# Turning both residuals on VectorE instead of TensorE, in a one-core hybrid decoder block (Trainium2)

## The reference

```python
m = (sigmoid(ga) * (y_h @ w_branch_hgrn) + sigmoid(gb) * (y_a @ w_branch_dsa))
h = h + m @ w_out
u = rmsnorm(h, ffn_norm_w)
a = causal_dwconv(u @ w_ffn_gate, ffn_conv_w, ffn_conv_b)
h = h + (silu(a) * (u @ w_ffn_up)) @ w_ffn_down
return rmsnorm(h, final_norm_w)[:, N_META:]
```

## Time and profile before

| | us |
|---|---|
| median of 3 runs | 1599.75 (1599.56 to 1600.13) |
| the profiled execution | 1599.79 |
| its span | 1598.0 |
| PE busy | 1586.3 (99%) |
| DVE busy | 972.0 (61%) |
| ACT busy | 708.5 (44%) |
| POOL busy | 116.0 (7%) |
| DMA, mean | 182 GB/s |

### The profile page before, as it was taken

The page is one execution under the profiler, slowest core; times in us unless marked ns, Lnnn a source line. Parts: engine busy times, 40 slices in busy tenths (PEclk is TensorE's granted clock), DMA queues, the critical chain, the costliest instruction groups (busy, mean ns, idle before and its releaser), DMA issues.

```text
span 1598.0 us, 29335 instructions
## 1 busy us (share of the span) xinstructions
PE 1586.3 (99%) x12162; PEld 1527.7 (96%) x12162; DVE 972.0 (61%) x1126; ACT 708.5 (44%) x746; POOL 116.0 (7%) x165
## 2 busy tenths in 40 slices
PE   9999999999999999999999999999999999999998
PEld 8999999999999999999999999998889999999886
DVE  7655878853355566786656666665445666666453
ACT  6433554544443345654345455544333334334342
POOL 1000140000000002352220000000000000000000
PEclk9999999999999999999999999999999999999999
DMA  7755555555555553576555565645455555565551
GB/s 244 227 179 164 158 165 179 178 179 179 179 189 180 159 159 119 191 246 203 177 191 191 172 195 165 203 162 204 173 198 181 188 180 187 174 194 198 196 210 54
DMA packets 244998, 290.36 MB, mean 182 GB/s; under 512 B 5697, under 2 KB 231218, under 8 KB 244530
## 3 DMA queue, kind: packets, MB, share of 16 engines
q1 hardware_dynamic: 238146, 278.78, 53.4%
q0 software_dynamic: 2176, 6.34, 1.2%
q10 hardware_dynamic: 4608, 4.23, 0.8%
HBM read 283.02 MB, written 6.32 MB: 181 GB/s over the span
## 4 chain that ended last, share of the span: by engine, by line
PE 99%; DVE 0%; ACT 0%; DMA 0%; issue 0%; SPq 0%; DVEq 0%
PE ps L654 25%; PE ps L655 24%; PE ps L656 24%; PE ps L1092 5%; PE ps L1095 5%; PE ps L1094 5%; PE ps L1041 2%; PE ps L1039 2%; PE ps L1040 2%; PE ps L817 1%; PE ps L685 0%; PE ps L792 0%; PE ps L934 0%; PE ps L1031 0%; PE ps L827 0%; PE ps L1079 0%
## 5 line engine op out<-in xcount | busy, mean ns | idle before, releaser
L654 PE MATMUL ps<-u_hi,w_hi 128*128 128x258 f32 (+2 forms) x2936 | 839.1, 286 | 0.0
L655 PE MATMUL ps<-u_lo,w_hi 128*128 128x258 f32 (+2 forms) x2936 | 831.4, 283 | 0.0
L656 PE MATMUL ps<-u_hi,w_lo 128*128 128x258 f32 (+2 forms) x2936 | 831.1, 283 | 0.0
L1447 DVE TENSOR_TENSOR w_lo<-raw,w_hi 128x2048 fp32r<-128x2048 f32 x259 | 598.1, 2309 | 353.6 <-ACT w_hi L1136 353.1
L1136 ACT ACTIVATE w_hi<-raw 128x2048 fp32r<-128x2048 f32 x259 | 495.9, 1916 | 565.1 <-PE ps L656 393.4
L654 PEld LDWEIGHTS ps<-u_hi,w_hi 128*128 128x128 f32 x2936 | 554.0, 189 | 5.1 <-DVE z_qf L1560 2.5
L655 PEld LDWEIGHTS ps<-u_lo,w_hi 128*128 128x128 f32 x2936 | 554.0, 189 | 0.3
L656 PEld LDWEIGHTS ps<-u_hi,w_lo 128*128 128x128 f32 x2936 | 553.8, 189 | 0.0
L1092 PE MATMUL ps<-w_hi,hid_hi 128*128 128x512 f32 x352 | 137.8, 391 | 0.0
L1095 PE MATMUL ps<-w_lo,hid_hi 128*128 128x512 f32 x352 | 137.1, 389 | 0.0
L1094 PE MATMUL ps<-w_hi,hid_lo 128*128 128x512 f32 x352 | 137.0, 389 | 0.0
(11 more groups left out here) (299 smaller groups left out, 1307.4 us busy)
## 6 DMA issues: line engine op xcount, KB each, us to landing
raw<-in_w_in_dram SPq DMA_DIRECT2D x47, 2048.0 KB, 8.5
raw<-in_w_ffn_gate_dram SPq DMA_DIRECT2D x22, 2048.0 KB, 8.1
raw<-in_w_ffn_up_dram SPq DMA_DIRECT2D x22, 2048.0 KB, 8.1
raw<-in_w_ffn_down_dram SPq DMA_DIRECT2D x20, 2048.0 KB, 7.6
raw<-in_w_out_dram SPq DMA_DIRECT2D x8, 2048.0 KB, 8.9
raw<-in_w_branch_hgrn_dram SPq DMA_DIRECT2D x8, 1024.0 KB, 5.5
raw<-in_w_branch_dsa_dram SPq DMA_DIRECT2D x8, 1024.0 KB, 8.8
gate_spill<-gate_st ACTq DMA_DIRECT2D x32, 129.0 KB, 3.9
```

What stands on the lines that cost most here:

```text
L654: mm(acc, w_hi[s][:, k, :], mov_hi(k), start=(k == first), stop=False)
L655: mm(acc, w_hi[s][:, k, :], mov_lo(k), start=False, stop=False)
L656: ins = mm(acc, w_lo[s][:, k, :], mov_hi(k), start=False, stop=(k == last))
L1447: v.tensor_tensor(w_lo[m % 4][:], raw[(m // 2) % 2][:, :, P * (m % 2):P * (m % 2) + P], w_hi[m % 4][:].bitcast(F32), ALU.subtract).then_in ...
```

## The change

Four things are edited.

1. **x is turned by DVE.** DMAs bring x as 32x32 blocks placed so that DVE's 32x32 block transpose gives the whole turn (`x_sh`, 16 DMAs of 32x8x32 for four units, `x_quad`; the two meta tokens as `xm_sh`, 4 DMAs). `x_sh[1]` lies over `ya_hi`, so its first load waits for the end of `U_MERGE`. PE's 48 turning matmuls go, and DVE adds bank and turned x in place of the copy.
2. **h is turned back by DVE.** DVE block-transposes each unit of h into a ring of four (`h_sh`); ACT stores it, one unit later, with 4 DMAs of 32x8x32 to a DRAM tensor `h_spill` that then holds h with tokens as rows. POOL loads it into `h_tok` after the stage, and DVE adds it at the end of the first `U_DOWN`. PE's 32 turning matmuls go.
3. **Merge entry.** ACT takes two sigmoids ahead of the weights, DVE takes the first sum ahead of the weight rest. The merge and out loops of ACT, DVE and POOL are written out instead of looped.
4. **Start.** ACT rounds the key panel's halves at n = 10 and 15 instead of 14 and 16, DVE makes the first rest at n = 12 instead of 15, the first half of the first query unit is rounded after the last x piece, and PE has one more warm-up matmul.

```diff
-        x_st = [at(f"x_st{a}", BIAS + 3072 * a, [P, 3, 256]) for a in range(2)]
+        x_sh = [at(f"x_sh{a}", (BIAS, R[4])[a], [P, 4, SEQ]) for a in range(2)]
+        xt = [at(f"xt{a}", BIAS + 4096 + 1024 * a, [P, SEQ]) for a in range(2)]
+        xm_sh = at("xm_sh", R[7] + 5184, [P, KT, 32])
...
+        x_blocks = x[0].rearrange("(b j) (k a i) -> a j k b i", j=32, a=4, i=32)
+        meta_blocks = meta_tokens.rearrange("j (k a i) -> a j k i", a=4, i=32)
+        h_blocks = h_spill.rearrange("(b j) (k a i) -> a j k b i", j=32, a=4, i=32)
...
+            def x_quad(q):
                 for a in range(4):
+                    for k in range(4):
+                        pool.dma_start(x_sh[q % 2][32 * a:32 * a + 32, k, :].rearrange("j (b i) -> j b i", i=32),
+                                       x_blocks[a, :, 4 * q + k, :, :]).then_inc(x_sh_in[q % 2], 16)
...
+            pool.wait_ge(o_gated, HEADS)
+            steps.link(pool, pool.memset(ssq[:], 0.0))
+            pool.wait_ge(projected, U_MERGE)
+            pool.wait_ge(ya_ready, 9)
+            pool.memset(xm_sh[:], 0.0).then_inc(xm_zeroed, 1)
+            x_quad(0)
+            pool.wait_ge(xm_zeroed, 1)
+            for a in range(4):
+                pool.dma_start(xm_sh[32 * a:32 * a + 2, :, :], meta_blocks[a, T0:META, :, :]).then_inc(xm_in, 16)
+            pool.wait_ge(projected, U_OUT)
+            x_quad(1)
+            for n in range(16):
+                if n in (4, 8):
+                    pool.wait_ge(xt_turned, n)
+                    x_quad(n // 4 + 1)
                 if n == 15:
                     pool.tensor_copy(spare[:, 5:6], ssq[:, 0:1]).then_inc(ssq_ready, 1)
                 squares(n, slice(n, n + 1), n == 15)
...
+            warm_up(1)
...
-                    if u % 2 == 0:
-                        pe.wait_ge(x_st_in[u // 2], 32 * i + 32)
                     pe.wait_ge(out_free, 4 * i + (u + 1))
-                    bank = ps[6 + u % 2]
-                    for t in range(3):
-                        ins = mm(bank[:, P * t:P * t + P], x_st[u // 2][:, t, P * (u % 2):P * (u % 2) + P], ident[:],
-                                 is_transpose=True, start=(t == 0), stop=False, skip_group_check=True)
-                    ins.then_inc(xt_turned, 1)
...
-                        if f == 0 and half == 0:
-                            residual(c, j % 2, t)
...
-                if n == 2 * EARLY:
+                if n == EARLY + 3:
                     act.wait_ge(key_in, 16)
                     round_keys(slice(0, 8))
-                if n == 2 * EARLY + 2:
+                if n == 2 * EARLY + 1:
...
+            gate_sigmoid(0)
+            gate_sigmoid(1)
+            ahead(U_MERGE)
+            for n in range(16):
+                ahead(U_MERGE + n + 1)
+                act.wait_ge(m_sum, n + 1)
...
+            def store_turned(u):
+                act.wait_ge(h_turned, u + 1)
+                for a in range(4):
+                    act.dma_start(h_blocks[a, :, u, :, :],
+                                  h_sh[u % 4][32 * a:32 * a + 32, :].rearrange("j (b i) -> j b i", i=32))\
+                        .then_inc(h_out[u % 4], 16)
...
+            for u in range(16):
+                m, h = U_OUT + u, h_res[:, u, :]
+                if u == 0:
+                    dve.wait_ge(xm_in, 64)
+                    v.transpose(xm[:].rearrange("p k t -> p (k t)"), xm_sh[:].rearrange("p k t -> p (k t)"))\
+                        .then_inc(xm_turned, 1)
+                    dve.wait_ge(xm_turned, 1)
+                if u % 4 == 0:
+                    dve.wait_ge(x_sh_in[(u // 4) % 2], 256 * (u // 8) + 256)
+                v.transpose(xt[u % 2][:], x_sh[(u // 4) % 2][:, u % 4, :]).then_inc(xt_turned, 1)
+                dve.wait_ge(xt_turned, u + 1)
+                dve.wait_ge(projected, m + 1)
+                v.tensor_tensor(h[:, 0:2], ps[6 + u % 2][:, 0:2], xm[:, u, 0:2], ALU.add)
+                v.tensor_tensor(h[:, 2:TQ], ps[6 + u % 2][:, 2:TQ], xt[u % 2][:], ALU.add).then_inc(out_free, 1)
...
+                v.transpose(h_sh[u % 4][:], h[:, 2:TQ]).then_inc(h_turned, 1)
+                ahead(m + 1, m + 1)
```

More of the change, by code:

```diff
@@ L339, in hybrid_block @@
         m_ready = sem("m_ready")
-        x_st_in = [sem("x_st_in0"), sem("x_st_in1")]
+        x_sh_in = [sem("x_sh_in0"), sem("x_sh_in1")]
+        xm_zeroed = sem("xm_zeroed")
+        xm_in = sem("xm_in")
+        xm_turned = sem("xm_turned")
         xt_turned = sem("xt_turned")
+        h_turned = sem("h_turned")
+        h_out = [sem(f"h_out{a}") for a in range(4)]
+        h_in = sem("h_in")
         ssq_ready = sem("ssq_ready")
@@ L601, in _ @@
                 gate_pair(n, n)
[L602 to L606, removed]
+            for n in range(4):
                 scale_gates(n, 16)
[L608 to L613, removed]
-                for a in range(4):
[L615 to L620, removed]
+            for n in range(4, 16):
+                pool.wait_ge(m_ready, n - 3)
+                gate_pair(n, n % 4)
+                if n > 4:
+                    scale_gates((n - 1) % 4, 16 * ((n - 1) // 4) + 16)
+            scale_gates(3, 64)
+            def x_quad(q):
+                for a in range(4):
+                    for k in range(4):
+                        pool.dma_start(x_sh[q % 2][32 * a:32 * a + 32, k, :].rearrange("j (b i) -> j b i", i=32),
+                                       x_blocks[a, :, 4 * q + k, :, :]).then_inc(x_sh_in[q % 2], 16)
             def squares(n, tile, last=False):
@@ L644, in _ @@
                 squares(n, slice(n, n + 1), n == 15)
+            pool.wait_ge(u2h_ready, 16)
+            pool.wait_ge(u2l_ready, 16)
+            for a in range(4):
+                pool.wait_ge(h_out[a], 4 * 64)
+            pool.wait_ge(ssq_ready, 2)
+            for c in range(2):
+                pool.dma_start(h_tok[c][:], h_spill[:, 1024 * c:1024 * c + 1024].rearrange("(t p) n -> p t n", p=P))\
+                    .then_inc(h_in, 16)
         @block.tensor
@@ L1037, in _ @@
                             pe.wait_ge(m_ready, k + 1)
[L1038 to L1042, removed]
+                        ins = products(ps[6 + u % 2][:, 0:TQ], n % 4, (k,), lambda k: m_hi[:, k, :],
+                                       lambda k: m_lo[:, k, :])
                     ins.then_inc(projected, 1)
@@ L1822, in _ @@
                         if u == 3:
+                            if half == 0:
+                                for r in range(4):
+                                    dve.wait_ge(h_out[r], 4 * 64)
                             low(0)
@@ L1849, in add @@
                     bank = ps[down_bank(half, c, u, t)][:].rearrange("p (g c) -> p g c", c=P)
-                    if half == 0:
-                        v.tensor_copy(h, bank).then_inc(down_added, 1)
-                    else:
-                        v.tensor_tensor(h, bank, h, ALU.add).then_inc(down_added, 1)
+                    v.tensor_tensor(h, bank, h, ALU.add).then_inc(down_added, 1)
                 for j in range(1, FH - 3):
```

108 lines of the change are left out of this document (42 added, 66 removed).

## The result

| us | before | changed |
|---|---|---|
| median | 1599.71 (1599.56 to 1600.13, 6 runs) | 1588.92 (1588.72 to 1589.34, 6 runs) |
| span of the profiled execution | 1598.0 | 1587.0 |
| PE / DVE / POOL busy | 1586.3 / 972.0 / 116.0 | 1576.2 / 978.5 / 146.8 |

The ratio is 0.9932, interval 0.9922 to 0.9943: 10.8 us faster. The prediction said 1594.3 (5.5 faster) and a range that began at 1589.0, 0.1 us above the result.

A forecast was written before the change was run, and what follows sets the result against it. PE, 99% busy with almost no stall to win, was taken as the bound. Terms -8.8 - 0.5 + 1.8 + 2.2 - 0.2 = -5.5 us on 1599.79 gave 1594.3, range 1589 to 1600.5.

The forecast's parts named there:

- Turns taken off PE, -8.8: Out and first down stages: 16 turns of x at 0.33 us and 8 banks of h at 0.44 save 8.8 us.
- Merge entry, -0.5: Merge start: PE's 1.1 us stall goes, 0.6 is given back for second release and late panel; net -0.5 us.
- the second release: Merge entry: two weight rests delay the second bank's release to 668.2, while PE asks at 668.0.
- the late panel: Merge entry: SyncE's next weight panel leaves 2.4 us later; 0.6 us given back for this and the second release together.
- The first sum, +1.8: Out stage: x loads land late, the first sum frees its bank at 756.7, PE asks at 754.9: 1.8 us stall.
- The loop and the `ssq` matmul, +2.2: Out stage: VectorE's loop takes 5.7 us a unit, so PE waits 2.2 us at the sum-of-squares matmul.
- Start, -0.2: Kernel start: the wait for the keys' first rest goes against x pieces held up by the earlier rounding; -0.2 us.
- a part of a rival: Start, within "All is hidden": the added matmul brings PE's quicker turning pace sooner, saving 0.8 us.
- All is hidden: Rival, out stage: meta tokens land early or the loop takes 5.45, no stall comes; 1589.7 to 1590.3 us, chance 0.2.
- POOL's issues: Rival, ahead of the first sum: x loads cost more than 0.79 us an issue; about 1607 at 1.6, chance 0.08.
- The DMA engines: Rival, out stage: 28,672 small pieces fill the DMA engines and panels come late, deciding at 24 ns each; chance 0.07.
- VectorE was not the bound: Rival, out stage: VectorE's loop takes 6.1 us, the last sum comes 6 us later; about 1600 us, chance 0.15.

The follow-up runs named there:

- e3: The changed kernel with the merge entry as before (weight roundings and rest ahead of the first sigmoid and sum): 1589.63 us.
- e11: The changed kernel with 9 more clearings of the meta buffer on POOL ahead of the first loads of x: 1595.49 us.
- e4: The changed kernel with 16 more clearings of the meta buffer on POOL ahead of the first loads of x: 1599.07 us.
- e6: The changed kernel with the block transpose of x done twice in each output-stage unit: 1594.82 us.
- e1: The changed kernel without the one added warm-up matmul: 1589.46 us.
- e2: The changed kernel with the key panel rounded and split where it was before, the added warm-up matmul kept: 1589.12 us.
- e8: The changed kernel with a second store of each turned unit of h, by POOL into another DRAM tensor: 1603.69 us.

## Why the prediction was wrong

The profiled execution was 11.0 us shorter, the forecast said 5.5. Of the 5.5 between them 4.0 are two waits that did not come, 0.8 the turns, 0.5 the start and 0.2 the merge entry.

- **Turns taken off PE, -8.8: right, sized too small.** By the traces 5.72 and 3.85, together 9.6; by the runs 9.5. The 0.33 and 0.44 of the chain are the turns' own starts. The distance between the same matmul of two units, 6.12 against 5.76, shows 0.36 for x, and the down stage 0.48 a bank.
- **Merge entry, -0.5: nearly right.** 0.73 by the trace, 0.5 by e3. The stall went as worked out, the second release cost its 0.2, and the 0.4 for the late panel did not come.
- **The first sum, +1.8: this is the step that failed.** POOL's issue was priced at 0.79 by a load over 128 partitions; the load over 32 took 0.58. Over 16 issues that is 3.3 us. The scaling ended 1.6 us sooner than reckoned, in part since start and merge had gained more, and the landing took 4.8 instead of 6.0. VectorE's own part took 1.3 us for the 1.15 assumed. Together the first sum came 5.9 us sooner than predicted (750.3 for 756.15): not 2 us late but with 3.2 us in hand. e11 and e4 show the slack, and the price once it is spent.
- **The loop and the `ssq` matmul, +2.2: the loop was right, the wait was not.** 5.7 us a unit were predicted and 5.62 taken where PE didn't set the pace (e11); the block transpose took 0.44 for the 0.45 assumed. But the 2.2 us were inherited from the late first sum. From 750.3 on, the same loop ends its last sum at 835.3, and PE's `ssq` matmul finds it ready. e6 shows that with 0.4 us more a unit the predicted wait is there, 2.0 us.
- **Start, -0.2: too small.** 0.7 in the profiled execution. The prediction saw this as a part of a rival, 0.8 by the quicker pace come sooner, and took it for unlikely. It is there in some executions (e1), and worth about 0.3 in the median. The key rounding, for which the 0.2 stood, showed no difference in the runs (e2).
- **The rivals.** "All is hidden" is what happened: 1589.7 by its terms, 1588.9 with the pace. It had a chance of 0.2, because the stall was taken as a sum of middle values, while its own bounds went to 0. POOL's issues proved cheaper and not dearer. The DMA engines didn't fill up (13 ns a packet against 24). VectorE was not the bound, but is 0.14 us a unit from it on the mean (5.62 against 5.76). By the Trainium skill (VectorE: DVE Perf Modes, "The three transpose paths") the prediction had an estimate of 0.62 a unit; the trace has 0.44 for 128x256 float32, and the measurement decides. With 0.62 the loop would take an estimated 5.8, just over PE's 5.76 and well short of e6's 6.04.
- **A fault the result hides.** The forecast added its two waits at their bare lengths. e11, e4, e6 and e8 show that waits of 4.7, 7.8, 2.0 (behind one of 1.1) and 12.3 us also take the clock down behind them, for 1.5 to 2.3 us more, and that in e11 this loss covers the second wait. Whether a first wait of the predicted 1.8 us would have cost the clock no run shows, so it stays open whether the forecast would have been too low for a late first sum.

## What to carry to other kernels

Where the tensor engine has no wait, instructions taken from it come in whole; what decides is whether the helper's first result is in time, since a helper whose loop is as full as the main engine's carries its lateness to the end of the stage. Price the DMA issues ahead of that first result by a row of the same shape, and give the issue queue a range of its own: here 128 partitions took 0.79 an issue and 32 took 0.58, but the rows differ in the size of the pieces too, and no run separates the two. A stall can be dearer than its length, when TensorE's clock falls in it.

## What the runs showed of the hardware

- POOL issued loads of 32 partitions x 8 pieces of 128 B at 0.58 us each, of two rows of the meta tokens at 0.60, against 0.79 and 0.54 in the earlier trace rows. An issue of ScalarE for the same shape took 0.47 (median).
- VectorE's block transpose of float32 took 0.44 us for 128x256 and 0.71 for 128x512.
- A POOL square of 0.63 us took up to 2.33 beside VectorE's two-input subtraction (e8), and that subtraction 2.75 instead of 2.29 when POOL's squares were under way first (changed kernel).
- TensorE's clock fell to its lower level in waits of 4.7, 7.8 and 12.3 us and came back 5.1, 3.1 and 3.7 us after work began again (e11, e4, e8). At the end of a wait of 2.0 us behind one of 1.1 it fell too (e6); in one of 1.1 us alone it did not. What activity decides this these runs don't show.
